# Sum of squares of the compressed query: the two squared chunks added on GpSimd, then one product with ones instead of two

## What is computed

```
def rms_norm(x, g):
    xf = x.astype(jnp.float32)
    return (xf * lax.rsqrt(jnp.mean(xf * xf, axis=-1, keepdims=True) + RMS_EPS)).astype(x.dtype) * g

def token_mixer(...):                       # once in each of DEPTH = 2 layers
    proj = h @ w_in
    qa, ka, va, iq, ik, iw, cq, ckv, kr, ga, gb = jnp.split(proj, split_at, axis=-1)
    ya = dsa_attention(...iq, ik, iw...)    # index scores choose keys
    q = (rms_norm(cq, q_norm_g) @ w_uq)...
    kv = (rms_norm(ckv, kv_norm_g) @ w_ukv)...
    ...
```

## Time and profile before

| | |
|---|---|
| time, median of 3 runs | 2347.01 us (2345.16 to 2347.82) |
| span of the profiled execution | 2343.6 us; no time of its own beside the span is recorded for it |
| PE busy | 2304.0 us, 98% |
| PEld, DVE, ACT, POOL busy | 79%, 54%, 43%, 43% |
| chain of work that ended last, by engine | PE 80%, issue 10%, POOL 4%, DVE 3% |

### The profile page before, as it was taken

One profiled execution on the slowest core, in us unless ns is written; L12 is line 12 of the kernel. 1 busy time (PEld: TensorE's weight loads), 2 busy tenths in 40 slices (PEclk: granted clock), 3 DMA queues, 4 the chain that ended last, 5 costly groups with the idle time before them and its releaser, 6 DMA issues.

```text
span 2343.6 us, 32209 instructions
## 1 busy us (share of the span) xinstructions
PE 2304.0 (98%) x11370; PEld 1855.9 (79%) x11370; DVE 1265.8 (54%) x2670; ACT 996.8 (43%) x1665; POOL 1016.7 (43%) x908
## 2 busy tenths in 40 slices
PE   7999999999999999999999999999999999999998
PEld 4778878888888887888788888888888877788767
DVE  8675775843445367668576444315540163185684
ACT  7454455344433244544524434423142354333473
POOL 3452223454444453423144444445454434455472
PEclk9999999999999999999999999999999999999999
DMA  9632144323226344213442222223322221222210
GB/s 347 246 112 73 47 129 149 126 90 107 89 78 242 110 184 151 80 37 115 137 162 90 90 95 102 81 92 115 107 90 89 100 84 36 90 90 90 90 46 37
DMA packets 51846, 259.57 MB, mean 111 GB/s; under 512 B 6352, under 2 KB 16080, under 8 KB 26128
## 3 DMA queue, kind: packets, MB, share of 16 engines
q1 hardware_dynamic: 50576, 249.63, 30.8%
q0 software_dynamic: 1152, 8.39, 0.9%
HBM read 249.47 MB, written 7.34 MB: 110 GB/s over the span
## 4 chain that ended last, share of the span: by engine, by line
PE 80%; issue 10%; POOL 4%; DVE 3%; ACT 1%; DMA 1%; SPq 0%; POOLq 0%; DVEq 0%; ACTq 0%
PE bank L750 23%; PE bank L752 22%; PE bank L751 22%; POOL w_lo L603 4%; PE bank L1006 2%; PE bank L914 1%; PE bank L1011 1%; PE bank L1261 1%; PE bank L903 1%; PE bank L1048 1%; PE bank L889 1%; DMA ada_early<-w_ada 1%; PE bank L1250 1%; PE bank L1415 1%; PE bank L864 0%
## 5 line engine op out<-in xcount | busy, mean ns | idle before, releaser
L603 POOL TENSOR_TENSOR w_lo<-w_raw,w_hi 128x512 fp32r<-128x512 f32 (+2 forms) x732 | 879.1, 1233 | 1158.3 <-ACT w_hi L1467 773.2
L750 PE MATMUL bank<-h_hi,w_hi 128*128 128x512 f32 x1616 | 645.4, 399 | 2.8 <-POOL w_lo L647 2.0
L752 PE MATMUL bank<-h_hi,w_lo 128*128 128x512 f32 x1616 | 630.4, 390 | 0.0
L751 PE MATMUL bank<-h_lo,w_hi 128*128 128x512 f32 x1616 | 629.4, 390 | 0.0
L750 PEld LDWEIGHTS bank<-h_hi,w_hi 128*128 128x128 f32 x1616 | 303.9, 188 | 69.7 <-issue 8.3
L752 PEld LDWEIGHTS bank<-h_hi,w_lo 128*128 128x128 f32 x1616 | 303.3, 188 | 65.0
L751 PEld LDWEIGHTS bank<-h_lo,w_hi 128*128 128x128 f32 x1616 | 304.0, 188 | 58.4 <-issue 1.0
L1467 ACT ACTIVATE w_hi<-w_raw 128x2048 fp32r<-128x2048 f32 (+2 forms) x108 | 190.0, 1760 | 276.2 <-PE bank L752 255.0
L2364 DVE SCALAR_TENSOR_TENSOR cv<-bank,par,cv 128x511 f32<-128x511 f32 (+1 forms) x176 | 131.7, 749 | 212.9 <-ACT cv L1737 199.9
L1472 ACT ACTIVATE w_hi<-w_raw 128x2048 fp32r<-128x2048 f32 x68 | 130.0, 1911 | 125.5 <-PE bank L752 117.0
L1737 ACT ACTIVATE cv<-bank,par 128x512 f32<-128x512 f32 x88 | 68.5, 780 | 233.0 <-PE bank L752 231.6
(11 more groups left out here) (378 smaller groups left out, 3847.2 us busy)
## 6 DMA issues: line engine op xcount, KB each, us to landing
w_raw<-w_stream SPq DMA_DIRECT2D x150, 1024.0 KB, 4.9
w_raw<-w_down SPq DMA_DIRECT2D x32, 704.0 KB, 4.0
ada_mid<-w_ada SPq DMA_DIRECT2D x20, 1024.0 KB, 5.4
ada_last<-w_ada SPq DMA_DIRECT2D x12, 1024.0 KB, 4.9
ada_early<-w_ada POOLq DMA_DIRECT2D x8, 1024.0 KB, 16.1
ada_late<-w_ada SPq DMA_DIRECT2D x8, 1024.0 KB, 6.3
bias_in<-bias_scratch SPq DMA_DIRECT2D x16, 256.0 KB, 3.1
bias_in<-bias_scratch SPq DMA_DIRECT2D x16, 192.0 KB, 2.7
```

Source lines behind the costliest of these rows:

```text
L603: ins = nc.gpsimd.tensor_tensor(w_lo[r][:, part], w_raw[r][:, part], w_hi[r][:, part].bitcast(fp32), ALU.subtract)
L750: nc.tensor.matmul(out, w[0][:, cols], xh, start=first, stop=False)
L751: nc.tensor.matmul(out, w[0][:, cols], xl, start=False, stop=False)
L752: return nc.tensor.matmul(out, w[1][:, cols], xh, start=False, stop=last)
```

## The change

- POOL's loop over slots 2 to 7 is cut in two. After slots 2 to 5 POOL waits for the layer's first two squares and adds `c_sq[1]` to `c_sq[0]`, in place, signalling the new semaphore `c_pair`; then it does slots 6 and 7.
- PE's `c_squares(1)` is gone. `c_squares(0)` is one product over the sum; it waits for `c_pair`, and for all three squares of the layer instead of the first. `c_squares(2)` is as before, apart from flags of the same meaning.
- ACT's two waits count two products a layer instead of three.

```
             for l in range(DEPTH):
                 n = slot_no(l, 0)
-                lo_loop(n + 2, SLOT_UQ - 2, SLOT)
+                lo_loop(n + 2, 4, SLOT)
+                pool.wait_ge(c_sqd, 3 * l + 2)
+                nc.gpsimd.tensor_tensor(c_sq[0][:, :], c_sq[0][:, :], c_sq[1][:, :], ALU.add).then_inc(c_pair, 1)
+                lo_loop(n + 6, SLOT_UQ - 6, SLOT)
                 lo(n + SLOT_UQ)
...
                 def c_squares(j):
-                    pe.wait_ge(c_sqd, 3 * l + j + 1)
+                    pe.wait_ge(c_sqd, 3 * l + 3)
                     pe.wait_ge(tile_evac, tdone(l, TILE_IDX + 7))
+                    if j == 0:
+                        pe.wait_ge(c_pair, l + 1)
                     if j == 2:
                         pe.wait_ge(c_stdd, 2 * l + 1)
-                    nc.tensor.matmul(banks[2][:, :], ones, c_sq[j][:, :], start=(j != 1), stop=(j != 0)
-                                     ).then_inc(c_ssq, 1)
+                    nc.tensor.matmul(banks[2][:, :], ones, c_sq[j][:, :], start=True, stop=True).then_inc(c_ssq, 1)
...
                     if u == 0:
                         c_squares(0)
-                        c_squares(1)
...
-                        act.wait_ge(c_ssq, 3 * l + 2)
+                        act.wait_ge(c_ssq, 2 * l + 1)
...
-                        act.wait_ge(c_ssq, 3 * (l + 1))
+                        act.wait_ge(c_ssq, 2 * (l + 1))
```

More of the change, by code:

```diff
@@ L304, in build @@
         c_sqd = sem("c_sqd")
+        c_pair = sem("c_pair")
         c_ssq = sem("c_ssq")
```

## The result

The changed kernel took 2357.12 us (median of 4 runs, 2355.51 to 2360.78); the kernel before, timed beside it, 2346.09 us (median of 4, 2343.8 to 2347.82). The ratio is 1.0049 with a 95% interval of 1.0037 to 1.0061: slower by 0.5%, 11.0 us by the medians. One of the 21 runs of the kernel before that stand beside three of the experiments took 8400.86 us and is left out of their ratios.

A forecast was written before the change was run, and what follows sets the result against it. PE was taken to bound the kernel. Net waits of 7.4 us plus 2.6 us for clock falls in both layers made 10.0 us, added to the median 2347.0 us: 2357.0 us, range 2353.0 to 2361.0 us.

The forecast's parts named there:

- What bounds it: Whole kernel: PE, busy 98% of the span, sets the end; its visible waits at the stage are 1.3 us.
- The product saved: PE, each layer: one fp32 product with ones less saves 0.86 us, 1.72 us in both layers.
- The wait: PE's product with ones, each layer: 4.34 us standing still for POOL's addition, plus 0.24 us restart, 4.58 us.
- The net loss at full clock: PE, each layer: wait and restart 4.58 us less 0.86 us saved, 3.72 us; 7.4 us in both.
- The addition's length and DVE: POOL behind slot 5: addition takes 1.29 us, starting before DVE's operation, which is the one stretched; upper end 1.72 us.
- The clock: PE at the new wait: the clock falls to its lower level in both layers, 2.6 us in all; chance 0.50.
- the sum that leaves it out: Both layers' waits without any clock fall: the sum ends at 7.4 us instead of 10.0 us.
- the price of a fall: PE's products at the lower clock at the wait: 1.3 us a layer, between 0.8 and 1.6 us.
- rival 4: More lost: stretched addition, loop end, dearer falls, 2358.9 us; with one more slow stretch a layer 2362.1 us; chance 0.07.
- A clock that stays up: Rival: PE waits but its clock stays up in both layers, 2354.4 us; chance 0.20.
- The loss given back by DVE or others: Rival: later in the stage, engines such as DVE pace PE and the delay vanishes, 2345.3 us; chance 0.06, fully or partly.
- The addition in time: Rival: POOL's addition is done before PE arrives at 94.49 us, so the gain is real, 2345.3 us; chance 0.01.

The follow-up runs named there:

- the last experiment: The change with the addition ahead of slot 5's low parts on POOL and PE's product with ones one gate step later: 2344.81 us, ratio 0.9997.
- the wait was filled: The change with 18 or 17 throwaway products on PE ahead of the product with ones: 2355.85 us, ratio 1.0038, and 2354.25 us, ratio 1.0035.
- the addition alone: The kernel before plus an addition at the change's place on POOL into a spare tile, which nobody waits for: 2346.58 us, ratio 1.0001.
- the wait without the saving: The change with both products with ones kept; PE still waits for the addition, whose sum goes to an unread tile: 2360.31 us, ratio 1.0059.
- the second execution: The same changed kernel, unedited, timed and traced again: 2357.79 us, ratio 1.0054 to the kernel before.
- the later product: The change with PE's product with ones behind the gate steps of u = 1, five steps later: 2346.91 us, ratio 1.0004.

## Why the prediction was right

The median came out 0.1 us from the forecast. The mechanism was right, but that closeness is luck: one term was too small and the start of the sum too high, as the last points say. Point by point:

- **What bounds it.** Right: PE met the wait in full, and nothing between the two stages gave it back. With the wait and the clock's part taken away, what is left is the product saved.
- **The product saved**, 0.86 us a layer. Right: the last experiment gains 0.86 and 0.87 us.
- **The wait.** Forecast 4.34 us, measured 4.18 and 4.17 us. The hand-over was 0.14 us as in the earlier trace rows, the addition 1.27 us against 1.29 us in the earlier trace rows, and POOL's loop end cost nothing visible: the addition follows slot 5 without a gap. The restart of 0.24 us is seen as 1.10 us for a product worth 0.86 us where the wait was filled.
- **The net loss at full clock.** Forecast 3.72 us a layer, measured 3.62 to 3.65 us.
- **The addition's length and DVE.** Right, with the order as argued: the addition came first and kept its time, DVE's operation took 1.32 us instead of 0.68 us. That is what the lock of "SBUF — State Buffer" in the Trainium skill, section "Who interferes with whom", says of the second comer. It cost nothing: the stage with the addition alone is that of before.
- **The clock.** Right that it falls in both layers; the waits of 4.2 us brought it down in all six cases traced (the change twice, the wait without the saving, two layers each), the waits of 2.95 us in one of two, and those of 1.73 us and less in none. So here the trace sides with the clock gate of "TensorE: Matmul & The Clock Gate" in the Trainium skill, Part 1, against the sum that leaves it out.
- **The step that was mis-sized: the price of a fall.** I put it at 1.3 us, between 0.8 and 1.6 us, from the one slow stretch of the earlier trace rows, which is 3.4 us long. Behind the waits of the change the stretch was about twice as long, 6.8 us in both layers. It cost 2.3 and 2.25 us, and in the second execution, with 6.8 us in both layers too, 2.8 and 2.5 us. I had named a fall that lasts twice as long as an unlikely case of rival 4; it is the normal one here. The stage therefore lost 11.65 us where I had 10.0.
- **Why the number still fits.** The metric moved by 11.0 us in the first series and by 12.2 us in the second. Measured against a before of 2346.09 us instead of the 2347.01 us that I started from, the forecast of +10.0 us is 1 to 2 us short. The start was 0.9 us too high and the loss 1.0 us too small in the first series, so the two errors cancel.
- **A reading that was wrong, without effect.** The 3.4 us between span and median were put down to what surrounds a span. Every run whose span is recorded takes 1.8 us more than it (2355.51 against 2353.7 us for the change); the rest is that the profiled execution of the kernel before was a quick one. The forecast adds to the median, so nothing hangs on it.
- **The rivals.** A clock that stays up would have given +7.4 us; it is excluded by the traces of both executions. The loss given back by DVE or others: excluded, the lengthened stage shows in the span, and the way from layer 0's stage to layer 1's is not shortened. The addition in time, and with it the gain, exists: it is the kernel with the addition ahead of slot 5 and the product one step later.

## What to carry to other kernels

When work is moved to an idle engine to relieve the one that sets the end, its price isn't its duration but the instant at which that engine, in its own order, gets to it, against the instant at which the bound engine asks for the result; here 1.27 us of addition cost 4.2 us of PE, to save 0.86 us. Read both instants from the timelines and place both ends: moving the addition ahead of a slot, or the product by a few steps, made the loss vanish or nearly so (-0.25 and +0.18 us a layer). And a standstill of PE of some 4 us costs more than itself, as the products behind it run at half clock; a wait of 2.95 us did this in one of two cases here, and one of 1.73 us in neither.

## What was not expected of the hardware

- Behind a full standstill of 4.2 us the clock stayed at its lower level for 6.8 us in five of six cases, though PE worked without a gap for the last 4.7 to 5.9 us of it. The sixth was 3.4 us long, like the one behind the tiny products at 813 us and the one behind a 2.95 us wait.
- The clock also falls at places that have nothing to do with the edit, in some executions of a kernel and not in others: at 813 us in the kernel before, at 468 us in the change and at 41 us in its second execution, at 40 and 1252 us with the later product, at 2257 us with the addition ahead of slot 5, nowhere before the end in the last version. The places recur. Of the twelve traces eight have a fall between 39 and 46 us, five between 463 and 471 us, three between 1251 and 1266 us, and five one or two between 2245 and 2273 us. Each of these places has thin work of PE just ahead of it, in the executions without a fall there too: at 813, 468 and 1252 us a row of products with 32 columns (32 of them in 3.65 us, 16 in 1.87 us, 16 in 1.87 us), at 39 to 46 us products with one column and standstills of 1.4 and up to 1.8 us, at 2245 to 2273 us a standstill of 1.5 us.
- A slow stretch of 3.4 us costs 1.6 us in an unbroken row of products, and 0.1 to 0.4 us at 468 us. The 1.6 us are of the size of the scatter between runs of one kernel, and of the whole gain that this change was after. A yardstick between two fixed points of the trace told differences of 0.2 us that the times could not.
